# Attention's value product with the values stationary, and the rotary half swap by transfers from GpSimd

## What is computed

```
logits = q k^T * 64^-0.5 + (c_q - c_k), causal
probs  = softmax(logits)
y_att  = probs v
merged = sigmoid(ga) * (y_att @ w_out_att) + sigmoid(gb) * (y_conv @ w_out_conv)
```

```
t1, t2 = t[..., :32], t[..., 32:]
out = concat([t1 * cos - t2 * sin, t1 * sin + t2 * cos])
```

## Time and profile before

| what | value |
|---|---|
| median of 3 runs | 1617.76 us (1616.62 to 1618.76) |
| the profiled execution | 1616.73 us |
| its span | 1615.0 us |
| busy in the span | PE 97%, weight loads 78%, DVE 56%, ACT 48%, POOL 7% |
| the attention with its projections | about 40 to 300 us |
| the retention with its projections | about 770 to 1040 us |

### The profile page before, as it was taken

One profiled execution on the slowest core, in us unless ns is written; L12 is line 12 of the kernel. 1 busy time (PEld: TensorE's weight loads), 2 busy tenths in 40 slices (PEclk: granted clock), 3 DMA queues, 4 the chain that ended last, 5 costly groups with the idle time before them and its releaser, 6 DMA issues.

```text
span 1615.0 us, 19990 instructions
## 1 busy us (share of the span) xinstructions
PE 1562.0 (97%) x7623; PEld 1262.7 (78%) x7623; DVE 898.0 (56%) x1114; ACT 773.8 (48%) x925; POOL 119.5 (7%) x95
## 2 busy tenths in 40 slices
PE   6999999999999899989899999999999999999998
PEld 5767777888787678868688888887886788888887
DVE  5434334345578788977553453544365655555565
ACT  6554445323557688856544333454134443443334
POOL 1101001000022233310010000000000000000000
PEclk9999999999989999999999999999999999999999
DMA  4457463224099999842412121222331323333221
GB/s 152 144 179 247 169 224 130 79 95 134 27 324 353 344 357 361 320 156 79 149 55 76 53 77 52 90 79 69 143 102 52 105 87 106 95 98 106 81 85 72
DMA packets 179857, 230.42 MB, mean 143 GB/s; under 512 B 12730, under 2 KB 151286, under 8 KB 176463
## 3 DMA queue, kind: packets, MB, share of 16 engines
q1 hardware_dynamic: 171712, 216.95, 39.6%
q0 software_dynamic: 7600, 12.41, 2.1%
q10 hardware_dynamic: 479, 0.16, 0.0%
HBM read 226.52 MB, written 18.37 MB: 152 GB/s over the span
## 4 chain that ended last, share of the span: by engine, by line
PE 84%; DVE 5%; ACT 4%; DMA 3%; issue 3%; ACTq 0%; POOL 0%; DVEq 0%; POOLq 0%
PE psum L459 21%; PE psum L461 20%; PE psum L460 20%; DMA hg<-h_rows,at_row 2%; PE psum L1885 2%; PE psum L1887 2%; PE psum L1886 2%; PE psum L775 1%; DMA y_rows<-y_sb,at_row 1%; PE psum L857 1%; ACT w_hi L432 1%; DVE pre L539 1%; PE psum L1912 1%; PE psum L1861 1%; PE psum L1913 1%
## 5 line engine op out<-in xcount | busy, mean ns | idle before, releaser
L459 PE MATMUL psum<-h_hi,w_hi 128*128 128x512 f32 x1160 | 462.6, 399 | 9.2 <-DVE w_lo L436 3.6
L460 PE MATMUL psum<-h_lo,w_hi 128*128 128x512 f32 x1160 | 453.2, 391 | 0.0
L461 PE MATMUL psum<-h_hi,w_lo 128*128 128x512 f32 x1160 | 453.1, 391 | 0.0
L436 DVE TENSOR_TENSOR w_lo<-raw,w_hi 128x2048 fp32r<-128x2048 f32 (+1 forms) x98 | 222.4, 2270 | 232.2 <-ACT w_hi L432 232.2
L459 PEld LDWEIGHTS psum<-h_hi,w_hi 128*128 128x128 f32 x1160 | 218.6, 188 | 68.5 <-issue 17.4
L461 PEld LDWEIGHTS psum<-h_hi,w_lo 128*128 128x128 f32 x1160 | 218.5, 188 | 46.7
L460 PEld LDWEIGHTS psum<-h_lo,w_hi 128*128 128x128 f32 x1160 | 218.9, 189 | 44.2 <-issue 1.4
L432 ACT ACTIVATE w_hi<-raw 128x2048 fp32r<-128x2048 f32 (+2 forms) x99 | 186.1, 1879 | 67.6 <-PE psum L461 64.5
L489 ACT ACTIVATE sq<-x 128x512 f32<-128x512 f32 x56 | 35.2, 631 | 142.3 <-DVE x L1379 81.7
L1833 DVE TENSOR_TENSOR w_lo_more<-raw_more,w_hi_more 128x2048 fp32r<-128x2048 f32 x34 | 77.8, 2287 | 23.3 <-ACT w_hi_more L1826 14.1
L1833 DVE TENSOR_TENSOR w_lo<-raw,w_hi 128x2048 fp32r<-128x2048 f32 x34 | 77.7, 2285 | 10.1 <-ACT w_hi L1826 7.2
(11 more groups left out here) (427 smaller groups left out, 2584.7 us busy)
## 6 DMA issues: line engine op xcount, KB each, us to landing
raw<-in_w_up SPq DMA_DIRECT2D x67, 512.0 KB
wm_raw<-in_w_mod SPq DMA_DIRECT2D x24, 1024.0 KB, 5.9
raw<-in_w_in SPq DMA_DIRECT2D x18, 1024.0 KB
raw<-in_w_in SPq DMA_DIRECT2D x33, 512.0 KB
raw_more<-in_w_down SPq DMA_DIRECT2D x24, 512.0 KB
raw<-in_w_gate SPq DMA_DIRECT2D x23, 512.0 KB
raw_more<-in_w_gate SPq DMA_DIRECT2D x22, 512.0 KB
raw_more<-in_w_up SPq DMA_DIRECT2D x22, 512.0 KB
```

What stands on the lines that cost most here:

```text
L436: dve.tensor_tensor(w_lo[j][:, 0:tiles, :], raw[j][:, 0:tiles, :], w_hi[j][:, 0:tiles, :].bitcast(F32), ALU.subtract).then_inc(G["lo_ready ...
L459: pe.matmul(to, w_hi[j][:, tile, :], hi_k, start=(k == 0), stop=False)
L460: pe.matmul(to, w_hi[j][:, tile, :], lo_k, start=False, stop=False)
L461: return pe.matmul(to, w_lo[j][:, tile, :], hi_k, start=False, stop=last)
```

## The change

Attention. `prob_v` makes the product the other way round: for each key block the values of a head (128 keys, 64 columns) are stationary and 128 columns of turned probabilities move; head 0 writes partitions 0 to 63 and head 1 partitions 64 to 127 of the same columns of the bank `Y`. The result has the channel on the partition at once, and `turn_y` goes, with its two waits. The row sums' reciprocals must now lie along the row: `invert` writes each reciprocal 64 times (in the buffer of `k_raw`), and two matmuls of `prob_v`, after a wait for them, spread them over the partitions, by an identity, beside the product. `y_norm` copies that to `y_tok` and multiplies it by the product; `y_hi` and `y_lo` read `y_tok`. `invert(m, 0)` goes ahead of the weight split of its place.

Retention. The matrix `turn`, its two matmuls and PE's wait for them go. GpSimd swaps the halves by eight SBUF-to-SBUF transfers a pair, of 32 partitions and 2 KB each, from `kr_raw` and `qr_raw` to `pre`; the sign is in the table `sin`. `rotate` waits until all eight have landed, and reads the swapped part in SBUF.

```diff
         def prob_v(pe, m, u):
+
             pe.wait_ge(M["m_prob_copied"], 4 * m + u + 1)
             if u == 0:
                 pe.wait_ge(M["m_v_tok"], m + 1)
-            if u == 0 or not isinstance(m, int):
-                pe.wait_ge(M["m_y_lo"], 4 * m + u + 1)
             if not (isinstance(m, int) and m == 0 and u == 0):
                 pe.wait_ge(M["m_y_tok"], 4 * m + u)
+            y, by = slice(0, P), slice(P, 2 * P)
+            for b in range(u + 1):
+                for h in range(2):
+                    pe.matmul(psum[64 * h:64 * h + 64, Y, y], v_tok[:, b, 64 * h:64 * h + 64],
+                              prob_t[:, h, b * P:(b + 1) * P], start=(b == 0), stop=(b == u))
+            pe.wait_ge(M["m_inv"], 4 * m + u + 1)
             for h in range(2):
-                for b in range(u + 1):
-                    done = pe.matmul(psum[:, Y, 64 * h:64 * h + 64], prob_t[:, h, b * P:(b + 1) * P],
-                                     v_tok[:, b, 64 * h:64 * h + 64], start=(b == 0), stop=(b == u))
+                done = pe.matmul(psum[64 * h:64 * h + 64, Y, by], row_inv[:, u, h, :], ident, start=True, stop=True)
             done.then_inc(M["m_y"], 1)
-
-        def turn_y(pe, m, u):
-            pe.wait_ge(M["m_y_tok"], 4 * m + u + 1)
-            pe.wait_ge(M["m_y_lo"], 4 * m + u + 1)
...
             def y_hi(m, u):
-                act.wait_ge(M["m_y_turned"], 4 * m + u + 1)
-                bank, cols = turned_y(m)
-                act.activation(d_hi[:, bass.ds(m, 1), u * P:(u + 1) * P], psum[:, bank:bank + 1, cols], ACT.Copy)\
+                act.wait_ge(M["m_y_tok"], 4 * m + u + 1)
+                act.activation(d_hi[:, bass.ds(m, 1), u * P:(u + 1) * P], y_tok[:, :].rearrange("p (o t) -> p o t", o=1), ACT.Copy)\
                    .then_inc(M["m_y_hi"], 1)
...
             def invert(m, u):
                 dve.wait_ge(M["m_prob"], 4 * m + u + 1)
-                dve.reciprocal(row_inv[:, u, :], row_sum[:, u, :]).then_inc(M["m_inv"], 1)
+                dve.reciprocal(row_inv[:, u, :, :], row_sum[:, u, :].rearrange("p (h o) -> p h o", o=1)
+                               .to_broadcast([P, 2, HEAD_DIM])).then_inc(M["m_inv"], 1)
 
             def y_norm(m, u):
                 dve.wait_ge(M["m_y"], 4 * m + u + 1)
-                dve.wait_ge(M["m_inv"], 4 * m + u + 1)
-                if not (isinstance(m, int) and m == 0 and u == 0):
-                    dve.wait_ge(M["m_y_turned"], 4 * m + u)
-                for h in range(2):
-                    done = dve.tensor_scalar(y_tok[:, 64 * h:64 * h + 64], psum[:, Y, 64 * h:64 * h + 64],
-                                             row_inv[:, u, h:h + 1], None, ALU.mult)
-                done.then_inc(M["m_y_tok"], 1)
+                dve.wait_ge(M["m_y_lo"], 4 * m + u + 1)
+                y, by = slice(0, P), slice(P, 2 * P)
+                dve.tensor_copy(y_tok[:, :], psum[:, Y, by]).then_inc(M["m_y_by"], 1)
+                dve.wait_ge(M["m_y_by"], 4 * m + u + 1)
+                dve.tensor_tensor(y_tok[:, :], y_tok[:, :], psum[:, Y, y], ALU.mult).then_inc(M["m_y_tok"], 1)
...
                 rest[3]()
-                pe.wait_ge(H["t_raw"], 4 * m + 2)
-                if not first:
-                    pe.wait_ge(H["t_state"], 14 * m)
-                pe.matmul(psum[:, SA, :], turn, kr_raw[:, 0:T], start=True, stop=True)
-                pe.matmul(psum[:, SB, :], turn, qr_raw[:, :], start=True, stop=True).then_inc(H["t_turn"], 1)
                 pe.wait_ge(H["t_raw"], 4 * m + 3)
                 context(1 - j, of_pairs, 1)
                 half_slot(pe, 1 - j, 1, of_pairs, 1)
 
                 rest[4]()
-                pe.wait_ge(H["t_qk"], 2 * m + 2)
+                if not first:
+                    pe.wait_ge(H["t_state"], 14 * m)
                 turn_v(m, 0, (SA, SB))
...
+                dve.wait_ge(H["t_turn"], 128 * m + 128)
+                dve.scalar_tensor_tensor(out=tmp, in0=tmp, scalar=scale, in1=sin, op0=ALU.mult,
                                          op1=ALU.mult).then_inc(H["t_rot"], 1)
...
+            def turn_heads(m):
+                for i, src in enumerate((kr_raw, qr_raw)):
+                    pool.wait_ge(H["t_raw"], 4 * m + i + 1)
+                    if m:
+                        pool.wait_ge(H["t_qk"], 2 * m - 1 + i)
+                    for q in range(4):
+                        pool.dma_start(pre[32 * (q ^ 1):32 * (q ^ 1) + 32, i, :], src[32 * q:32 * q + 32, 0:T])\
+                            .then_inc(H["t_turn"], 16)
+
+            turn_heads(0)
             pool.wait_ge(H["t_tab"], 1)
...
+            for m in range(1, 4):
+                turn_heads(m)
```

More of the change, by code:

```diff
@@ L120, in shape_constants @@
     blocks = np.kron(np.eye(2, dtype=np.float32), np.ones((64, 64), np.float32))
-    turn = np.zeros((P, P), np.float32)
-    for h in range(2):
-        for d in range(32):
-            turn[64 * h + 32 + d, 64 * h + d] = -1.0
-            turn[64 * h + d, 64 * h + 32 + d] = 1.0
+    sign = np.where(np.arange(P) % 64 < 32, -1.0, 1.0).astype(np.float32)[:, None]
     t = np.arange(T)
@@ L156, in shape_constants @@
         "tokens": np.tile(np.arange(T, dtype=np.float32)[None, :], (P, 1)),
-        "small": np.concatenate([ident, blocks, turn], axis=1),
-        "rope": np.stack([cos, sin], axis=1).reshape(P, 2 * T),
+        "small": np.concatenate([ident, blocks, ident], axis=1),
+        "rope": np.stack([cos, sign * sin], axis=1).reshape(P, 2 * T),
         "dft_d": dft_d,
@@ L886, in t1 @@
                 def t1():
-                    turn_y(pe, p, 1)
                     mods(2)
@@ L892, in t2 @@
                 def t2():
-                    turn_y(pe, p, 2)
                     mods(3)
                     prob_v(pe, p, 3)
-                def t3():
-                    turn_y(pe, p, 3)
-                return t0, t1, t2, t3
+                return t0, t1, t2, nothing
             def pair(m, rest):
@@ L1113, in y_lo @@
                 block = d_hi[:, bass.ds(m, 1), u * P:(u + 1) * P].bitcast(F32)
-                bank, cols = turned_y(m)
-                dve.tensor_tensor(d_lo[:, bass.ds(m, 1), u * P:(u + 1) * P], psum[:, bank:bank + 1, cols], block,
+                dve.tensor_tensor(d_lo[:, bass.ds(m, 1), u * P:(u + 1) * P], y_tok[:, :].rearrange("p (o t) -> p o t", o=1), block,
                                   ALU.subtract).then_inc(M["m_y_lo"], 1)
@@ L2531, in rotate @@
             def rotate(m, i):
-                raw_t, bank, out, scale = ((kr_raw, SA, kr_t, 1.0), (qr_raw, SB, qr_t, HEAD_DIM ** -0.5))[i]
+                raw_t, out, scale = ((kr_raw, kr_t, 1.0), (qr_raw, qr_t, HEAD_DIM ** -0.5))[i]
                 tmp = pre[:, i, :]
-                dve.scalar_tensor_tensor(out=tmp, in0=psum[:, bank, :], scalar=scale, in1=sin, op0=ALU.mult,
+                dve.wait_ge(H["t_turn"], 128 * m + 128)
+                dve.scalar_tensor_tensor(out=tmp, in0=tmp, scalar=scale, in1=sin, op0=ALU.mult,
                                          op1=ALU.mult).then_inc(H["t_rot"], 1)
```

18 lines of the change are left out of this document (5 added, 13 removed).

## The result

The changed kernel takes 1607.84 us in the median of 4 runs (1605.18 to 1609.07), the kernel before, on the same chip, 1618.26 us (1616.62 to 1620.81, 4 runs). The ratio is 0.9936, 95% interval 0.9924 to 0.9947: 10.4 us less by the medians.

A forecast was written before the change was run, and what follows sets the result against it. PE was taken to bound both changed stretches. Gains of 3.7 + 0.2 + 6.8 = 10.7 us took the profiled 1616.73 us to 1606.0; with 1.0 us for the median, the forecast was 1607.0 us, range 1602.5 to 1613.0.

The forecast's parts named there:

- The bound: In the attention and retention stretches PE sets the time: busy 242.1 of 245 us and 247.9 of 250 us.
- the stretch between: Rival: the stretch from 305 to 785 us absorbs the attention's gain, leaving the retention's 6.8 us, 1611 us; chance 0.10.
- The attention's products: Attention on PE: value products and turns of 18.9 us become 15.2 us with entries and exits, 3.7 us less.
- A full drain: Attention, tiling changes: draining TensorE fully would cost 4.6 us in place of 3.0, 1.6 us less gain.
- The satisfied waits: Attention: removed wait instructions gain nothing; bound 0.1 us each, 1.6 us in all, as `turn_y` with two waits stepped 0.11.
- The reciprocal: Attention on DVE: widened from 2 to 128 columns it takes about 1.5 us, in idle time, without PE waiting.
- The tail: Attention's end, last block to merge: the merge starts 0.8 us earlier, 0.6 already counted, so 0.2 us less.
- The retention's products: Retention on PE: two fp32 swap products go, 1.71 us a pair, 6.8 us less for four pairs.
- The swap's landing: Retention: GpSimd's transfers land some 8 us after `qr_raw` is written, nothing on the path; late-swap rival about 1647 us, chance 0.05.
- the prediction's sign: Retention, expected in the new profile: no PE wait for `kr_t`, and the swap landed before DVE's rotation.
- The room of 18 us: Retention: the swap may land up to about 875.0, 18 us after `qr_raw`, before lateness makes PE wait.
- The sum: Whole kernel: 3.7 + 0.2 + 6.8 = 10.7 us less.

## Why the prediction was right

- **The bound** held. What the traces show as taken from PE's stream, 10.4 us net, is what the medians show; each part alone gave a gain clear of zero, and the stretch between absorbed nothing beyond its own scatter of some microseconds.
- **The attention's products**, 18.9 to 15.2 us: the steps of 0.055, the entry of 0.09 and the exit of 0.15, all taken from the retention's product, fit the new blocks: from a block's start to the transposes behind it are 0.59, 0.81 (276.01 to 276.82) and 1.03 us (284.37 to 285.40) for 8, 12 and 16 instructions, which is 0.055 each and 0.15 once. The bank that both halves share was no hindrance. A full drain at the changes of tiling, the reading of the Trainium skill (TensorEngine Tiling (Array Packing), Key Properties) that the prediction weighed, would have given an estimated 0.16 and 0.22; the rows show the smaller gaps.
- **The satisfied waits** of the old code were priced at nothing. That was the attention's one miss: a gap of 0.3 us three times, at one place of the loop, that its reading of `turn_y` did not contain. With it 3.9 becomes 4.8.
- **The reciprocal** was sized at 1.5 us from 11 ns a column; it took 0.94, 6.3 ns a column from 2 to 128 columns. It made no difference, as said, because it was moved ahead of the split. Left where it stood it would have cost nearly the whole gain.
- **The tail**: from the turn ahead of the last block to the merge the chain of the kernel before had 3.44 us; from the last block's start it is 2.63 now, and 0.09 for the entry. That is 0.7 us less where 0.8 were forecast.
- **The retention's products**: 1.71 us a pair was exact in three pairs. In the first the term failed: the prediction took them off the path without asking what they had covered there. Behind them PE waits for both copies of the values; that wait is in the diff as an unchanged line, right under the removed ones. It gave back 1.2 us of the 6.8: 1.0 of idle time, and 0.2 at the start behind it.
- **The swap's landing** was sized at 8 us behind `qr_raw`; a q transfer issues in 0.50 us and lands in 2.1, so the four took about 4, and some 8 in the first pair (790.38 to 798.31), where the DMA share was 1.08 (792.5 to 796.2). There the swap landed behind the point where DVE was ready for it, against the prediction's sign, and PE lost nothing by it. The room of 18 us held as a lower bound: no loss with 12.6 us more; PE's own limit is 21.4 or a little more, and with 21 us more each pair lost 2.6 us.
- **The sum**, 10.7 us against 10.4, is closer than its terms, and that is luck: two misses of opposite sign, 0.9 us too little in the attention and 1.2 too much in the retention. Without the first the gain would have been 9.5.

## What to carry to other kernels

On an engine that is never idle, a gain is the count of removed steps times the start-to-start distance, taken from the same form elsewhere in the trace; what has to be searched for is what the removed work covered, that is, the next wait on the same engine behind it. Work for the two column halves should take turns, which is worth 3 us here. And a wait of one or two microseconds on PE is not priced by its length: see what the clock does behind it, and place the operation that it waits for, here the reciprocal, ahead of the long one in its queue.

## What the runs showed that I had not expected

- PE starts an instruction for an idle column half ahead of three earlier ones for the busy half, by the records of three blocks: without turns the block of eight loses nothing, that of twelve 0.27 us, that of sixteen 0.5.
- A wait of 1.6 to 1.8 us on PE was followed in three of four places by some three microseconds in which the granted clock was down in part (0.69, 0.66 and 0.71 over windows of 4 to 5 us): 2.3 us lost a place by the medians, not 1.8. Behind another wait, of 2.1 us, it fell in six of twelve traces and stayed in full in six.
- A satisfied wait in front of a matmul cost 0.46 us at one place of a loop and nothing at the others.
- A transfer of 64 KB inside SBUF from GpSimd: 0.50 us to issue, median 1.9 to 2.1 us to land, 6.4 at most, while weight loads ran. By the Trainium skill (DMA: Bandwidth & Descriptors, Anatomy of one DMA) a transfer takes a fixed 2.0 us and its bytes over 436 GB/s, an estimate of 2.15 us for this. The medians agree with it; but four in a row overlap and don't add up to the prediction's 8.6: with GpSimd held up they took 3.4 and 3.6.
